# Weight blocks and v as stationary operands in a hybrid decoder block: the convolution's columns and the attention's output come out turned

## The reference

```python
proj = jnp.einsum("bsd,de->bse", _rmsnorm(x, ln1_w[l]), w_in[l])
gdn_qkv, gdn_z, gdn_a, gdn_b, swa_qkv, gate_a, gate_b = _split_cols(proj)
# GDN branch: 8 heads of 128
qkv = jax.nn.silu(_causal_conv(qkv, conv_w))     # 4 taps along the tokens, for each channel
q, k = _l2norm(q) * HEAD_DIM ** -0.5, _l2norm(k)
o_a = gated_delta_rule(q, k, v, g, beta); ...
# attention branch: 3 groups of 4 heads, dilated windows
scores = jnp.where(valid, q @ k.T * HEAD_DIM ** -0.5, NEG_INF)
p = jnp.exp(scores - lse); o = p @ v             # the groups are merged by their lse
# both
mixed = sigmoid(gate_a) * (o_a @ w_gdn_proj) + sigmoid(gate_b) * (o_b @ w_swa_proj)
x = x + mixed @ w_out
x = x + square(relu(_rmsnorm(x, ln2_w[l]) @ w_ff1)) @ w_ff2
```

## Time and profile before

| | us |
|---|---|
| median of 3 runs | 1504.73 (1503.73 to 1505.4) |
| the profiled execution | 1504.53 |
| its span | 1502.7 |
| PE busy | 1495.5 |
| DVE busy | 1142.9 |
| ACT busy | 810.6 |
| POOL busy | 129.1 |

### The profile page before, as it was taken

One profiled execution on the slowest core, in us unless ns is written; L12 is line 12 of the kernel. 1 busy time (PEld: TensorE's weight loads), 2 busy tenths in 40 slices (PEclk: granted clock), 3 DMA queues, 4 the chain that ended last, 5 costly groups with the idle time before them and its releaser, 6 DMA issues.

```text
span 1502.7 us, 19550 instructions
## 1 busy us (share of the span) xinstructions
PE 1495.5 (100%) x7458; PEld 1259.1 (84%) x7458; DVE 1142.9 (76%) x1362; ACT 810.6 (54%) x917; POOL 129.1 (9%) x169
## 2 busy tenths in 40 slices
PE   9999999999999999999999999999999999999999
PEld 7888888888888888888888888888888888888887
DVE  6877756878777877776766777778989566578978
ACT  6555444676664544544444545456656445465654
POOL 6000000000041100100000112110000111110000
PEclk9999999999999999999999999999999999999999
DMA  8878897745545444445799888766877666666874
GB/s 292 216 256 296 301 342 265 236 160 168 171 166 165 144 140 148 145 154 197 264 322 324 272 285 297 249 224 218 302 263 266 193 188 194 193 219 217 306 290 146
DMA packets 156889, 345.37 MB, mean 230 GB/s; under 512 B 8336, under 2 KB 8848, under 8 KB 153488
## 3 DMA queue, kind: packets, MB, share of 16 engines
q1 hardware_dynamic: 148960, 317.09, 62.8%
q0 software_dynamic: 6592, 25.17, 4.7%
q10 hardware_dynamic: 1264, 2.13, 0.4%
HBM read 317.11 MB, written 27.26 MB: 229 GB/s over the span
## 4 chain that ended last, share of the span: by engine, by line
PE 90%; DVE 5%; DMA 3%; ACT 1%; issue 1%; SPq 0%; POOL 0%; ACTq 0%; DVEq 0%; POOLq 0%
PE banks L630 44%; PE banks L1007 16%; PE banks L1053 9%; PE banks L1010 8%; PE banks L1075 5%; DVE lo L2188 3%; DMA raw<-in_w_ff 2%; PE banks L646 1%; DVE t_sums L2219 1%; DMA early_sum<-in_w_ff 1%; PE banks L904 1%; PE banks L913 1%; PE banks L764 0%; PE banks L653 0%; PE banks L788 0%
## 5 line engine op out<-in xcount | busy, mean ns | idle before, releaser
L1569 DVE TENSOR_TENSOR lo<-raw,hi 128x1024 fp32r<-128x1024 f32 x383 | 471.6, 1236 | 254.4 <-ACT hi L1108 252.8
L1108 ACT ACTIVATE hi<-raw 128x1024 fp32r<-128x1024 f32 x383 | 404.6, 1059 | 437.8 <-PE banks L630 258.8
L630 PE MATMUL banks<-hi,st 128*128 128x512 f32 x1584 | 499.7, 397 | 0.1
L630 PEld LDWEIGHTS banks<-hi,st 128*128 128x128 f32 x1584 | 290.7, 189 | 54.8 <-DVE lo L1569 0.5
L1007 PE MATMUL banks<-st,hi 128*128 128x512 f32 x1024 | 321.6, 395 | 0.0
L630 PE MATMUL banks<-lo,st 128*128 128x512 f32 x792 | 309.6, 391 | 0.0
L1010 PEld LDWEIGHTS banks<-st,lo 128*128 128x128 f32 x1024 | 192.4, 188 | 45.4
L1519 ACT ACTIVATE hi<-raw 128x1024 fp32r<-128x1024 f32 x160 | 169.0, 1061 | 110.6 <-PE banks L1075 61.4
L2188 DVE TENSOR_TENSOR lo<-raw,hi 128x1024 fp32r<-128x1024 f32 x160 | 192.9, 1222 | 21.0 <-ACT hi L1519 15.2
L1010 PE MATMUL banks<-st,lo 128*128 128x256 f32 x1024 | 201.2, 278 | 0.0
L630 PEld LDWEIGHTS banks<-lo,st 128*128 128x128 f32 x792 | 149.4, 189 | 31.5
(11 more groups left out here) (312 smaller groups left out, 1646.6 us busy)
## 6 DMA issues: line engine op xcount, KB each, us to landing
raw<-in_w_ff SPq DMA_DIRECT2D x116, 1024.0 KB, 5.9
raw<-in_w_in SPq DMA_DIRECT2D x99, 1024.0 KB, 5.1
raw<-w_sums SPq DMA_DIRECT2D x24, 1024.0 KB, 5.1
raw<-in_w_out SPq DMA_DIRECT2D x16, 1024.0 KB, 7.4
early_sum<-in_w_ff SPq DMA_DIRECT2D x12, 1024.0 KB, 8.0
w_sums<-early_sum SPq DMA_DIRECT2D x12, 1024.0 KB, 9.4
late_sum<-in_w_ff POOLq DMA_DIRECT2D x12, 1024.0 KB, 5.9
w_sums<-late_sum POOLq DMA_DIRECT2D x12, 1024.0 KB, 5.5
```

What stands on the lines that cost most here:

```text
L630: last = pe.matmul(acc[:, t], x_t, v[:, (i + more) % PIECES, kk, :], start=m == 0 and kk == 0 and a == 0, stop=m == n - 1 and kk == 1 and ...
L1108: act.activation(hi[:, (i + more) % PIECES], raw[:, i // 2 % RAW, 2 * (i % 2):2 * (i % 2) + 2, :], ACT.Copy)\
L1569: dve.tensor_tensor(lo[:, (i + more) % PIECES], raw[:, i // 2 % RAW, 2 * (i % 2):2 * (i % 2) + 2, :], hi[:, (i + more) % PIECES].bitcast(F ...
```

## The change

The columns of gi = 0 to 5 are made turned at once. `turned_group` takes the 128 x 128 blocks of the weight pieces as stationary and 256 tokens of `st_hi` or `st_lo` as moving operand, so a PSUM bank holds 2 x 128 channels by 256 tokens, and there are twice as many matmuls of half the width. `b_turn`, `stage` and `b_xc` are gone. VectorE reads the banks into `xc` and multiplies them by the row factors, which now lie along the free dimension: `rstd1_row`, all 256 factors on every partition, by a third small DMA on POOL's queue. The taps move from m = 3 to 6 to m = 2 to 5.

In the attention v is the stationary operand, so the output comes out turned and `ob_turn` is gone. The row sums can then no longer be applied behind it; VectorE multiplies the probabilities by their reciprocals before they are turned (`w_scaled`, m = 2), TensorE's turning waits for that, and ScalarE copies the output into `o_b` (`w_out_`, m = 7). `w_ptr` and `w_pv` move from after half pairs 3 and 5 to after 4 and 6, and `w_pt` on ScalarE from m = 4 to m = 5.

```diff
+            def turned_group(q, g, after):
+                place = 0
+                for pair in range(4):
+                    for t in range(TT):
+                        for m in (2 * pair, 2 * pair + 1):
+                            if t == 0:
+                                pe.wait_ge(lo_ready, 8 * q + m + 1)
+                            if m == 0:
+                                pe.wait_ge(acc_free, 2 * g + 1 + t)
+                            for kk in range(2):
+                                for b in range(2):
+                                    at = P * (2 * t + b)
+                                    for a, (w, v) in enumerate(((hi, st_hi), (lo, st_hi), (hi, st_lo))):
+                                        last = pe.matmul(acc[:, t, TT * P * b:TT * P * b + TT * P],
+                                                         w[:, m % PIECES, kk, at:at + P], v[:, 2 * m + kk, :],
+                                                         start=m == 0 and kk == 0 and b == 0 and a == 0,
+                                                         stop=m == 7 and kk == 1 and b == 1 and a == 2)
...
@@ TensorE
-                    pe.wait_ge(ev["w_exp"], n + 1)
+                    pe.wait_ge(ev["w_o"], 2 * n + 2)
...
-                        last = pe.matmul(wk[:, 4, 0:P], pt[:, P * b:P * b + P], swa_v[:, kt, at:at + P],
+                        last = pe.matmul(wk[:, 4, 0:P], swa_v[:, kt, at:at + P], pt[:, P * b:P * b + P],
...
-                after = {0: w_sc(h, t), 3: w_ptr(h, t), 5: w_pv(h, t)}
-                if gi == 7:
-                    after[6] = ob_turn
+                after = {0: w_sc(h, t), 4: w_ptr(h, t), 6: w_pv(h, t)}
...
-                if 1 <= gi <= 6:
-                    after[1] = b_turn(gi - 1)
...
-                group(QB + gi, GB_ + gi, 8, st_hi, st_lo, after=after)
+                if gi < 6:
+                    turned_group(QB + gi, GB_ + gi, after)
+                else:
+                    group(QB + gi, GB_ + gi, 8, st_hi, st_lo, after=after)
@@ GpSimd
+                pool.dma_start(rstd1_row[:], r_rows.partition_broadcast(P)).then_inc(ev["r_moved"], 16)
@@ ScalarE
-                if 1 <= gi <= 6:
-                    steps[2] += [b_xc(n)]
...
-                steps[4] += [w_pt(h, t)]
+                steps[5] += [w_pt(h, t)]
+                steps[7] += [w_out_(h, t)]
@@ VectorE
+            def w_scaled(h, t):
+                n = 2 * h + t
+                def step():
+                    dve.wait_ge(ev["w_exp"], n + 1)
+                    dve.reciprocal(rsm[:, t:t + 1], sm[:, t:t + 1]).then_inc(ev["w_o"], 1)
+                    ts_(sc[:], sc[:], rsm[:, t:t + 1], None, ALU.mult, None, (ev["w_o"], 2 * n + 1), ev["w_o"])
+                return step
+            def conv_rows(gi):
+                def read(t):
+                    tt_(xc[:, 2 * t:2 * t + 2, CONV - 1:CONV - 1 + TT * P],
+                        acc[:, t].rearrange("p (b n) -> p b n", n=TT * P), bcast(rstd1_row[:], 1, [P, 2, TT * P]),
+                        ALU.mult, None, acc_free)
+                def first():
+                    if gi:
+                        dve.wait_ge(ev["b_conv"], 16 * gi)
+                    else:
+                        dve.wait_ge(ev["pad_made"], 1)
+                        dve.wait_ge(ev["r_moved"], 48)
+                    dve.wait_ge(acc0_done, GB_ + gi + 1)
+                    read(0)
+                def second():
+                    dve.wait_ge(piece_used, 8 * (QB + gi) + 8 + PIECES)
+                    read(1)
+                return first, second
...
-                        dve.wait_ge(ev["b_xc"], n + 1)
+                        dve.wait_ge(acc_free, 2 * (GB_ + n) + 4)
...
-                        steps[3 + j] += [b_conv(n, j)]
+                        steps[2 + j] += [b_conv(n, j)]
...
-                steps[6] += [w_out_(h, t)]
+                steps[2] += [w_scaled(h, t)]
...
-                ahead(QB + gi, 8, steps, more_steps=lambda m, gi=gi: stored_sums(8 * (QB + gi) + m))
+                ahead(QB + gi, 8, steps, read_out=conv_rows(gi) if gi < 6 else (),
+                      more_steps=lambda m, gi=gi: stored_sums(8 * (QB + gi) + m))
```

More of the change, by code:

```diff
@@ L134, in build_block @@
         swa_mask = sb("swa_mask", [P, 6, P], F32, 132)
-        o_b = sb("o_b", [P, TT, HS * P], F32, 140)
+        o_b = sb("o_b", [P, HS, TT * P], F32, 140)
         swa_qk = sb("swa_qk", [P, 2, NG * HS, TT * P], F32, 144)
@@ L640, in group @@
                             place += 1
+            def turned_group(q, g, after):
[15 more added lines that the diff above has]
+                                                         stop=m == 7 and kk == 1 and b == 1 and a == 2)
+                            if t == 1:
+                                last.then_inc(piece_used, 1)
+                            elif m == 7:
+                                last.then_inc(acc0_done, 1)
+                            if place % 2 and place // 2 in after:
+                                after[place // 2]()
+                            place += 1
             def turn(src, dst, done):
@@ L728, in _ @@
                           tokens=one_parity if g >= 6 else None)
[L731 to L742, removed]
             def b_ss(n):
                 def step():
-                    pe.wait_ge(ev["b_xc"], n + 2)
+                    if n:
+                        pe.wait_ge(ev["b_nl"], n)
+                    else:
+                        pe.wait_ge(ev["a_stored"], 6)
                     pe.wait_ge(ev["b_sqlo"], n + 1)
@@ L819, in g_sums, with both @@
                 pe.matmul(wk[:, 5, 16:32], ones[:], gg, start=True, stop=True).then_inc(ev["ab_products"], 1)
+            def both(*steps):
+                def step():
+                    for a in steps:
+                        a()
+                return step
             for gi in range(8):
@@ L830, in _ @@
                     after[7] = g_sums
[L831 to L832 removed]
                 if 2 <= gi <= 5:
[L834 to L835 removed]
+                    after[6] = both(after[6], b_ss(gi - 2))
+                if gi < 6:
+                    turned_group(QB + gi, GB_ + gi, after)
+                else:
+                    group(QB + gi, GB_ + gi, 8, st_hi, st_lo, after=after)
             W = [wk[:, 2 + n, :] for n in range(4)]
@@ L1250, in w_pt, with w_out_, step @@
                 return step
+            def w_out_(h, t):
+                def step():
+                    f(by_parity(o_b[:])[:, h, t], wk[:, 4, 0:P], ACT.Copy, (ev["w_pv"], 2 * h + t + 1), ev["w_ot"])
+                return step
             def both(*steps):
@@ L1305, in ob_hi_step @@
             def ob_hi_step():
-                f(by_parity(ob_hi[:]), by_tile(tbv), ACT.Copy, (ev["d_turned"], 1), ev["d_hi"])
+                f(ob_hi[:], o_b[:], ACT.Copy, (ev["w_ot"], 2 * HS), ev["d_hi"])
             def g_exps():
@@ L1337, in _ @@
                 steps = {m: both(*a) for m, a in steps.items() if a}
[L1338 to L1342, removed]
+                z_read = () if gi < 6 else read_out(QB + gi, GB_ + gi, 8, lambda t, a=4 * (gi - 6):
+                                                    zs[:, t, a:a + 4, :].rearrange("p h d -> p (h d)"))
+                ahead(QB + gi, 8, steps, read_out=z_read)
             def gate(g, cnt, which, i):
@@ L1766, in step @@
                     dve.wait_ge(ev["w_exp"], n + 1)
[L1767 to L1770, removed]
-                return step
+                    dve.reciprocal(rsm[:, t:t + 1], sm[:, t:t + 1]).then_inc(ev["w_o"], 1)
+                    ts_(sc[:], sc[:], rsm[:, t:t + 1], None, ALU.mult, None, (ev["w_o"], 2 * n + 1), ev["w_o"])
+                return step
+            def conv_rows(gi):
[6 more added lines that the diff above has]
+                        dve.wait_ge(ev["b_conv"], 16 * gi)
+                    else:
+                        dve.wait_ge(ev["pad_made"], 1)
[6 more added lines that the diff above has]
+                return first, second
             def b_conv(n, j):
@@ L1871, in ob_lo_step @@
             def ob_lo_step():
-                tt_(by_parity(ob_lo[:]), by_tile(tbv), by_parity(ob_hi[:].bitcast(F32)), ALU.subtract, (ev["d_hi"], 1), ev["d_lo"])
+                dve.wait_ge(ev["w_ot"], 2 * HS)
+                tt_(ob_lo[:], o_b[:], ob_hi[:].bitcast(F32), ALU.subtract, (ev["d_hi"], 1), ev["d_lo"])
             def g_consts():
```

31 lines of the change are left out of this document (9 added, 22 removed).

## The result

| | before | after |
|---|---|---|
| median, us | 1504.32 (1503.58 to 1506.94, 13 runs) | 1507.61 (1505.22 to 1508.33, 13 runs) |
| span of the profiled execution, us | 1502.7 | 1506.3 |

The ratio of after to before is 1.0019, 95% interval 1.0011 to 1.0026: 0.2% slower, 3.3 us by the medians. The forecast was +2.6 us on the profiled execution, which would be 1507.1 us; it took 1508.33.

The account below looks back on a forecast made before the run. TensorE was taken to bound the kernel, busy 1495.5 of 1502.7 us. Turns and their wait -6.7, short matmuls +4.8, bank waits +4.4, probabilities' turn +0.1 gave +2.6 on 1504.53: 1507.1, kept as 1507.0 us, range 1501.0 to 1511.5.

Parts of the forecast that it names:

- The turns: Seven turns on TensorE in the changed stage, 0.87 us each, go with a 0.6 us wait: -6.7 us together.
- The pace of the short matmuls: TensorE, first six groups: 576 matmuls of 512 columns become pairs of 256 at 117.5 ns, +4.8 us (0 to +9.4).
- VectorE's list sets the release of the bank: Group ends: TensorE waits for VectorE's in-order bank read, 19.7 us of list in full groups; new waits 4.4 us.
- The prediction's own balance: Full-group boundary: TensorE's wait S = 7.15 - S + 19.7 + 0.1 - 25.8, so 0.57 us.
- The two instructions of VectorE: VectorE: bank read 0.68 us; scaling 512 probabilities 0.39 us, 0.58 us with the reciprocal, against 0.46 us removed.
- The rule that ScalarE is closer to PSUM: It speaks against moving the bank read to VectorE; rows of 0.67 and 0.68 us show no price, none counted.
- The turn of the probabilities: Scaled probabilities come even with TensorE's need at 15.0 us; wait 0 to 0.2 us a group, 0.1 in all.
- The DMA of the row factors: POOL's third DMA, following one issued at 45.72 us, is first waited for later than 140 us: no cost.
- rivals 2 and 3: Short matmuls at 113.3 ns: banks late, +0.6, 1505.1 us, chance 0.08; banks in time, -6.7, 1497.8 us, chance 0.10.
- rival 1: Group ends: bank reads come in time with short matmuls at 117.5 ns: -1.9 us, 1502.6 us; chance 0.12.
- rival 4: Group boundaries: VectorE's list is the bound and longer than its parts; 1 us longer is +3.5, 1510.5 us; chance 0.22.
- rival 5: Short matmuls at 121.5 ns: +4.6 us, waits give back 2.8, so +4.4, 1508.9 us; chance 0.11.

Follow-up runs that it names:

- the experiment with two buffers: The whole change with two xc buffers in turn, VectorE reading bank 0 ahead of the last taps and the clamp: 1505.74 us, ratio 1.0007 to before.
- the cut kernel: The kernel before with each 512-column matmul of groups 0 to 5 cut in two of 256, same stationary block, nothing turned: 1510.22 us.
- two buffers and the early scaling: The whole change with two xc buffers, and probabilities scaled ahead of the silu product and first tap: 1504.68 us, ratio 1.0002 to before.

## Why the prediction was right, point by point

- **The turns.** Right. The attention part alone gives back the turn of `o_b`, its wait, and 0.2 us that the prediction had not counted: the wait for the exponentials in B2.
- **The pace of the short matmuls.** The mechanism was right, the size was not. The row taken was 32 matmuls at 117.5 ns; measured are 119.7 ns, so the term is 576 x (2 x 119.7 - 226.7) ns = +7.3 us and not +4.8. The value lies inside the bounds, near the upper one. In the trace of after the same 32 matmuls take 3.84 us, 120.0 ns, and so they do in every experiment; the row of before that carried the choice was the odd one out. Why it ran at 117.5 ns there is open.
- **VectorE's list sets the release of the bank.** Right: a longer list lengthens the waits, a shorter one shortens them, and a list with the read further ahead removes them. The working of the list holds too: in B3 it runs from the first split at 308.88 us to the end of the read at 328.46, 19.6 us against the 19.7 of the prediction. The size of the waits was too high, 4.4 us against 2.9, for the same reason as the term above: with 119.7 ns TensorE's own group is 0.42 us longer and gives VectorE that much more time. The prediction's own balance then says 1.5 us at B1, 0.4 at B2 and 0.36 at each of B3 to B5, 3.0 in all. So two terms that were off by +2.5 and -1.5 us hang together, and the sum moved by less than either.
- **The two instructions of VectorE.** The read took 0.68 us, as said. The scaling of 512 elements was listed with 0.49 us and followed after 0.40 us; with the reciprocal 0.60 us against the 0.58 of the sum.
- **The rule that ScalarE is closer to PSUM** (the Trainium skill, VectorE: DVE Perf Modes, section Specifications) made no difference here: the read has 683 ns on VectorE, and had 0.67 us on ScalarE. What the move cost was the place in VectorE's list.
- **The turn of the probabilities.** It waited nowhere in after, as said (0 to 0.2 us a group). That it was even there shows in the experiment with two buffers, where it waited 1.2 us.
- **The DMA of the row factors** cost nothing: POOL issued it at 47.49 us.
- **The rivals.** 113.3 ns (rivals 2 and 3) is out by the traces of after and of the cut kernel. Banks in time at 117.5 ns (rival 1) is what two buffers and the early scaling make of the kernel, at the measured pace: +0.3 us on the stage and not -1.9. A list longer than its parts (rival 4) did not occur. The experiment shows its price: 1.14 us more in each group made 4.2 us of waits, 3.7 us per us against the 3.5 of the prediction. The clock took 1.5 of the 5.8 us by which the stage grew, which the prediction had not thought of. The pace of 121.5 ns (rival 5) was nearer than the forecast's.

Sum by the measured terms: -6.1 (turns) - 0.8 (waits that went) + 7.3 (width) + 2.9 (banks) = +3.3 us, against 2.9 us measured on the stage. The difference lies where blocks of matmuls and small steps meet, which I counted as equal: the cut kernel has all the small steps of before, and there the width costs 6.7 us (6.5, and 0.2 for the wait that went) and not 7.3. With 6.7 the sum is +2.7 us.

That +2.6 was forecast and +2.9 measured is in part luck. The pace was 2.5 us too low and the waits 1.5 us too high, and these two hang together. But the 0.2 us of the exponentials and the 0.6 us of the meeting places were not in the prediction at all, and they happen to take away most of what was left.

## What to carry to other kernels

Before a turn is taken away by swapping the operands, look at the width of the new matmuls. Here two short ones cost 12.7 ns more than a wide one, and halving 576 of them cost 7.3 us by their pace (6.7 in the stage), more than the 5.2 us of the 48 transposes. And where a PSUM bank's reader moved to another engine, the duration of the read was not the price (0.68 us against 0.67); its place in that engine's list was. A second buffer, which let the read go ahead of the last taps, took the waits for banks away, and the scaling had to move ahead as well before all of it was gained. When a wait grows, look at the clock behind it too. Take a change apart before judging it: one half of this one gains 0.1%, the other loses 0.2%.

## What the runs showed of the hardware that was not expected

- A float32r matmul of this kernel, with a weight load for each, costs about 13 ns beside its columns at 2.4 GHz: 226.7 ns for 512 columns (213.3 by the columns alone) and 119.7 for 256 (106.7). Whether the float32r or the weight load makes the price was not separated.
- At the lower level of the clock this price does not show: with the granted clock at 0.50, 256 columns took 213 ns, which is what the columns alone take at 1.2 GHz (the kernel with the longer list).
- In the same kernel 2.7 us without work on TensorE were followed by 3.4 us at half the clock, which cost 1.5 us; the 1.6 us wait of after cost nothing of the kind.
- The Trainium skill, TensorE: Matmul & The Clock Gate, section Back-to-back issue gap, gives N/2.4 plus 2.5 ns for a matmul by itself, and says that in a stream with a weight load before each matmul both set the spacing. The prediction took the first and left out the second. By the first the cut would have cost 1.4 us; by their pace the short matmuls cost 7.3.
- Narrow matmuls are dearer than their columns say: if the wide one of a pair follows the law above, 192 and 128 columns cost about 110 and 113 ns (an estimate from the 256.7 and 286.7 ns of the pairs), though 93 and 67 would follow from the law and 109 is what transposes take.
- The starts that a trace gives for matmuls of changing width don't show each one's own time: the next start comes 59 ns after one of 128 columns and 228 ns after one of 384. A pace has to be read over several.
